# Out projection of the two attention mixers started inside their attention tails, with a split first addition, one filler less per stage and fillers in two other attentions

## The reference, cut to what matters

```python
h = rms_norm(x, norm_mix_pre[layer])
h = neighbourhood_attention(h, ...) if layer % 2 == 0 else dilated_attention(h, ...)
x = x + rms_norm(h, norm_mix_post[layer])       # attention ends with o @ w_o
h = rms_norm(x, norm_ffn_pre[layer])
x = x + rms_norm(swiglu(h, ...), norm_ffn_post[layer])
```

## Time and profile before

| | |
|---|---|
| median of 3 runs | 2242.76 us (2242.03 to 2244.25) |
| the profiled execution, its own time | 2243.23 us |
| its span, first to last instruction | 2241.4 us |
| TensorE busy | 2105.5 us, 94% |
| VectorE busy | 1391.8 us, 62% |
| ScalarE busy | 948.2 us, 42% |
| mean granted TensorE clock | 0.963 of full speed |
| moved from HBM | 338.82 MB, 152 GB/s over the span |

### The profile page before, as it was taken

One profiled execution on the slowest core, in us unless ns is written; L12 is line 12 of the kernel. 1 busy time (PEld: TensorE's weight loads), 2 busy tenths in 40 slices (PEclk: granted clock), 3 DMA queues, 4 the chain that ended last, 5 costly groups with the idle time before them and its releaser, 6 DMA issues.

```text
span 2241.4 us, 37080 instructions
## 1 busy us (share of the span) xinstructions
PE 2105.5 (94%) x15038; PEld 1942.8 (87%) x15038; DVE 1391.8 (62%) x1849; ACT 948.2 (42%) x1258; POOL 31.9 (1%) x48
## 2 busy tenths in 40 slices
PE   7989999999989999999998988999999995789998
PEld 6869988999969998998997877998899894688997
DVE  5747755655646765774667555775577456575763
ACT  4444444333444444443443334544444332544442
POOL 0000000000000000000000000000000000000000
PEclk9989999999999999999997879999999997988999
DMA  7324554343414554555530124455455552142552
GB/s 281 138 85 169 187 197 175 135 171 132 150 58 159 187 197 150 189 187 197 204 126 1 57 85 160 147 191 194 152 188 187 197 184 94 48 150 88 191 196 107
DMA packets 49788, 341.46 MB, mean 152 GB/s; under 512 B 5776, under 2 KB 6544, under 8 KB 9616
## 3 DMA queue, kind: packets, MB, share of 16 engines
q1 hardware_dynamic: 45216, 321.21, 39.6%
q10 hardware_dynamic: 4464, 18.68, 2.3%
HBM read 338.82 MB, written 1.05 MB: 152 GB/s over the span
## 4 chain that ended last, share of the span: by engine, by line
PE 83%; DVE 12%; ACT 3%; issue 2%; DMA 0%; POOL 0%; DVEq 0%; ACTq 0%; SPq 0%; POOLq 0%
PE pj L226 14%; PE pj L227 14%; PE pj L228 14%; PE acc L232 7%; PE acc L233 7%; PE acc L234 7%; DVE wlo L302 2%; PE pj L560 2%; PE pj L232 2%; PE pj L234 2%; PE pj L233 2%; PE acc L628 2%; ACT whi L295 1%; PE pj L566 1%; PE acc L616 1%
## 5 line engine op out<-in xcount | busy, mean ns | idle before, releaser
L302 DVE TENSOR_TENSOR wlo<-raw,whi 128x2048 fp32r<-128x2048 f32 x288 | 660.0, 2292 | 341.8 <-ACT whi L295 341.1
L226 PE MATMUL pj<-xh,whi 128*128 128x256 f32 x2704 | 772.6, 286 | 18.3 <-DVE wlo L312 13.4
L227 PE MATMUL pj<-xl,whi 128*128 128x256 f32 x2704 | 768.9, 284 | 0.0
L228 PE MATMUL pj<-xh,wlo 128*128 128x256 f32 x2704 | 768.9, 284 | 0.0
L295 ACT ACTIVATE whi<-raw 128x2048 fp32r<-128x2048 f32 x299 | 569.6, 1910 | 461.2 <-PE acc L234 230.9
L226 PEld LDWEIGHTS pj<-xh,whi 128*128 128x128 f32 x2704 | 522.5, 193 | 21.5 <-issue 16.0
L227 PEld LDWEIGHTS pj<-xl,whi 128*128 128x128 f32 x2704 | 522.4, 193 | 0.1
L228 PEld LDWEIGHTS pj<-xh,wlo 128*128 128x128 f32 x2704 | 522.3, 193 | 0.0
L232 PE MATMUL acc<-whi,AR 128*128 128x512 f32 x688 | 275.2, 400 | 6.7 <-DVE AR L1940 4.4
L233 PE MATMUL acc<-whi,AR 128*128 128x512 f32 x688 | 273.9, 398 | 0.0
L234 PE MATMUL acc<-wlo,AR 128*128 128x512 f32 x688 | 273.7, 398 | 0.0
(11 more groups left out here) (348 smaller groups left out, 2391.3 us busy)
## 6 DMA issues: line engine op xcount, KB each, us to landing
raw<-in_wstream SPq DMA_DIRECT2D x302, 1024.0 KB, 4.8
F<-in_gains ACTq DMA_DIRECT2D x12, 512.0 KB, 4.6
F<-in_rpb ACTq DMA_DIRECT2D x3, 1024.0 KB, 4.7
F<-in_memtok ACTq DMA_DIRECT2D x2, 1024.0 KB, 4.9
F<-in_memin ACTq DMA_DIRECT2D x2, 1024.0 KB, 7.0
F<-in_small ACTq DMA_DIRECT2D x1, 1536.0 KB, 10.5
F<-in_xin SPq DMA_DIRECT2D x2, 512.0 KB, 7.0
xt<-in_xtok SPq DMA_DIRECT2D x1, 1024.0 KB, 12.2
```

What stands on the lines that cost most here:

```text
L226: nc.tensor.matmul(o, wh, k_hi, start=first, stop=False, skip_group_check=True)
L227: nc.tensor.matmul(o, wh, k_lo, start=False, stop=False, skip_group_check=True)
L228: return nc.tensor.matmul(o, wl, k_hi, start=False, stop=last, skip_group_check=True)
L302: nc.vector.tensor_tensor(wlo[:, gs, :], raw[:, gs, :], whi[:, gs, :].bitcast(F32), ALU.subtract).then_inc(w_lo, 1)
```

## The change

In words: (a) in na and dil the sums of token half 0 go to `pj0` and `pj1` instead of `acc0` and `acc1` (`out_banks`), and the products of token half 0 with the first three weight chunks (input tiles 0 to 5, 6 matmuls each) are issued in `fill` after units 10 to 15; the fillers of these two stages are gone. The output projection then makes only banks 2 and 3 for chunks 0 to 2 (`early=3`) and all four for the last chunk. (b) `added(1, 0)` is two instructions, of 128 and of 384 columns; "x" counts 5 a stage, and TensorE turns block 0 of token half 1 after the first and blocks 1 and 2 after the second. (c) The last `keep_busy` ahead of the next stage's projection is left out. (d) `attn_pe` issues fillers in xa and dsa: ahead of each unit's transposes 3 matmuls in xa and 1 in dsa, and once after the scores of the second unit 6 and 2.

```diff
-            shares(f"s{s_}pre", "pre", {**NORM, "x": 4 if s_ else 0, "tr": KT if s_ else 0})
+            shares(f"s{s_}pre", "pre", {**NORM, "x": 5 if s_ else 0, "tr": KT if s_ else 0})
...
+        def out_banks(kind):
+
+            return [pj[0], pj[1], acc[2], acc[3]] if kind in ("na", "dil") else acc
...
-            def added(t, h):
+            def added(t, h, cols=slice(0, 512)):
                 dve.wait_ge(*at(tag, "rs", t + 1))
-                x = xt[:, t, h * 512:(h + 1) * 512]
-                nc.vector.scalar_tensor_tensor(x, tmp[2 * t + h], rsc[:, t:t + 1], x, ALU.mult, ALU.add)\
+                x = xt[:, t, h * 512:(h + 1) * 512][:, cols]
+                nc.vector.scalar_tensor_tensor(x, tmp[2 * t + h][:, cols], rsc[:, t:t + 1], x, ALU.mult, ALU.add)\
                     .then_inc(sg(nxt[0], "x"), 1)
...
-            added(1, 0)
+            added(1, 0, slice(0, P))
+            added(1, 0, slice(P, 512))
...
                 pe.wait_ge(*at(nxt, "x", 2))
-                for k in range(3):
+                turn_pe(pe, 1, 0).then_inc(sg(nxt, "tr"), 1)
+                pe.wait_ge(*at(nxt, "x", 3))
+                for k in range(1, 3):
                     turn_pe(pe, 1, k).then_inc(sg(nxt, "tr"), 1)
-                fill(pe, 4)
+                if fill is not keep_busy:
+                    fill(pe, 4)
...
-                    for b in range(4):
+                    for b in range(2 if c < early else 0, 4):
...
+        def idle(bank, n):
+
+            for _ in range(n):
+                nc.tensor.matmul(bank[:, 0:T], ident, cst[:, 0:T], start=True, stop=True)
...
             def transposes(u, U):
+                N = n_parts(U)
+                if N == 1 and u >= 2:
+                    pe.wait_ge(*at(tag, "pts", u - 1))
+                idle(parts(u, U)[0][0], U.get("idle", 0))
                 pe.wait_ge(*at(tag, "pn", u + 1))
...
             for i, U in enumerate(units):
+                if i == 0:
+                    idle(parts(u0, U)[0][0], U.get("lead", 0))
                 if i + 2 < len(units):
                     scores(u0 + i + 2, units[i + 2])
...
-                    if i >= 3 * UP:
-                        for _ in range(3 if na else 5):
-                            nc.tensor.matmul(pj[0][:, 0:T], ident, cst[:, 0:T], start=True, stop=True)
+                    if i >= 10:
+                        first_half(i - 10)
+
+                def first_half(kt):
+
+                    c, kk = divmod(kt, 2)
+                    gs = (w.g + c) % 3
+                    pe.wait_ge(w_lo, w.g + c + 1)
+                    pe.wait_ge(*at(tag, "od", kt + 1))
+                    for h in range(2):
+                        wk = slice(kk * D + h * 512, kk * D + (h + 1) * 512)
+                        mm3t(pj[h][:, :], whi[:, gs, wk], wlo[:, gs, wk], AR[:, kt, 0:P], AR[:, 8 + kt, 0:P],
+                             kt == 0, False)
...
-                out_pe(pe, w, 8, 8, tag, "od", nxt)
+                out_pe(pe, w, 8, 8, tag, "od", nxt, ob=out_banks(kind), early=3)
...
-                sp.wait_ge(*at("end", "x", i + 1))
+                sp.wait_ge(*at("end", "x", (1, 3, 4, 5)[i]))
```

More of the change, by code:

```diff
@@ L115, in build_program @@
             shares(f"s{s_}post", "post", {"g": 16, "ob": 3, "sq": 4, "mv": 2, "rs": 2})
-        shares("end", "pre", {"x": 4})
+        shares("end", "pre", {"x": 5})
         def sg(tag, n):
@@ L385, in pre_sq @@
             if tag != "s0pre":
-                act.wait_ge(*at(tag, "x", 4))
+                act.wait_ge(*at(tag, "x", 5))
             for t in range(2):
@@ L415, in post_act, with post_dve @@
                     act.wait_ge(w_used, w.g + 1)
-                nc.scalar.activation(JUNK[:, b * 512:(b + 1) * 512], acc[b][:, :], ACT.Square, accum_out=ss[:, b:b + 1])\
+                nc.scalar.activation(JUNK[:, b * 512:(b + 1) * 512], ob[b][:, :], ACT.Square, accum_out=ss[:, b:b + 1])\
                     .then_inc(sg(tag, "sq"), 1)
             act_phase(act, w, 1)
-        def post_dve(dve, w, tag, half, nxt):
+        def post_dve(dve, w, tag, half, nxt, ob):
             tmp = [Sb[:, 0, :], Sb[:, 1, :], PTb[:, 0, :], PTb[:, 1, :]]
@@ L425, in scaled @@
                 dve.wait_ge(*at(tag, "sq", b + 1))
-                link(dve, nc.vector.scalar_tensor_tensor(tmp[b], acc[b][:, :], half * D ** 0.5,
+                link(dve, nc.vector.scalar_tensor_tensor(tmp[b], ob[b][:, :], half * D ** 0.5,
                                                          GB[:, (b % 2) * 512:(b % 2 + 1) * 512], ALU.mult, ALU.mult))
@@ L473, in keep_busy, with out_pe @@
                 nc.tensor.matmul(mb[:, T:2 * T], ident, cst[:, 0:T], start=True, stop=True)
-        def out_pe(pe, w, nk, lo_at, tag, ready, nxt, beside=lambda pe, c: None, fill=keep_busy, kt0=0):
+        def out_pe(pe, w, nk, lo_at, tag, ready, nxt, beside=lambda pe, c: None, fill=keep_busy, kt0=0,
+                   ob=acc, early=0):
             post = tag + "post"
@@ L729, in two_heads @@
                              j == 0, j == 1) for a in range(2) for j in range(2)],
-                        nk=2 * T, H=2, soft=[soft(t)] * 2, grp=grp, per=2, end=t == 1)
+                        nk=2 * T, H=2, soft=[soft(t)] * 2, grp=grp, per=2, end=t == 1, idle=n_idle,
+                        lead=2 * n_idle)
         def split_out(tag, perm, o_bank):
@@ L1084, in xattn @@
                                lambda h, j: V[:, j, h * P:(h + 1) * P],
-                               lambda t: lambda S, ps: nc.vector.tensor_scalar(S, ps, P ** -0.5, None, ALU.mult), t, g)
+                               lambda t: lambda S, ps: nc.vector.tensor_scalar(S, ps, P ** -0.5, None, ALU.mult), t, g,
+                               3)
                      for g in range(2) for t in range(2)]
@@ L2134, in _ @@
                 fns[2](act, w)
-                post_act(act, w, f"s{s}post")
+                post_act(act, w, f"s{s}post", out_banks(kind))
                 if s + 1 < len(plan):
```

17 lines of the change are left out of this document (7 added, 10 removed).

## The result

The changed kernel takes 2214.38 us, the median of 4 runs (2213.06 to 2215.14), against 2243.01 (2242.03 to 2244.25) for the kernel before on the same chip: a ratio of 0.9871, with a 95% interval of 0.9856 to 0.9887. The forecast was 2215.0. Its profiled execution took 2214.05 us, 29.18 less than the 2243.23 of the profile before.

A forecast was written before the change was run, and what follows sets the result against it. TensorE, busy 94% of the span, was taken as the bound; 2243.23 - 9.5 (na) - 9.0 (dil) - 5.2 (stage ends) - 4.3 (xa) + 0.2 gave 2215.4, stated as median 2215.0. Range 2208 to 2222, with rivals 2203 to 2227.

The forecast's parts named there:

- the 8.4 us of each projection: na and dil: 36 matmuls of 0.233 us leave each output projection, bound by TensorE alone, saving 8.4 us.
- The margin at the last weight chunk: Output projection: last weight chunk ready at 7.4 us, wanted at 8.4 us, 1.0 us to spare.
- If the clock is back by about 124: na's tail: full clock by then starts the projection 1 to 2 us earlier; na gains 9.5, bounds 4.0 and 10.0.
- The two filler rows: na's tail: six filler passes take 2.56 us at 129.88 and 1.56 at 134.17, read as gapless work restoring the clock.
- dil, 0.9 gained and 0.3 lost: dil's tail: last packet brings 0.9 us forward, units 10 and 11 cost 0.3; with 8.4, dil gains 9.0.
- The stage ends: Nine stage ends: split addition and dropped filler save 0.58 us each, the filler's share 0.3; 5.2 us in all.
- both limits named: Stage end: the filler ends near 168.1, and ScalarE is busy with the chunk until 168.38.
- The fillers in xa: xa: leading fillers fill the 2.75 us idle; the second xa gains 4.3 us, the first 0; bounds 0 and 5.
- Forecast +0.1: dsa: fillers before the transposes are together 0.3 us too long, costing 0.1 us, at most 0.5.
- Rival 1: Second addition binds at stage ends (1.8 instead of 5.2) and second xa stays slow (0): 2222.6 us; 15%.
- Rival 3: Tails of na and dil: packets hold the clock at 0.50 through both, slower at 2252 us; 2%.
- Rival 2: Low-clock stretches elsewhere, as in rwrt, move, up to 14 us either way: 2207 (10%) or 2223 to 2229 (8%).

The follow-up runs named there:

- e1: The kernel before with part (a) alone: 2225.96 us.
- b1: The changed kernel with bank 2 also made early in dil, into `pj2`, 9 matmuls a packet instead of 6: 2215.28 us, ratio 0.9881.
- e7: The changed kernel with packets in units 12 to 15 only and two chunks early instead of three: 2215.49 us.
- e6: The kernel before with na's three fillers in units 10 and 11 too, dil as before: 2246.06 us.
- e2: The kernel before with the split addition alone, the filler ahead of the projection kept: 2240.86 us.
- e5: The changed kernel without the leading fillers of xa and dsa, those ahead of the transposes kept: 2217.04 us.
- e8: The changed kernel without any filler in dsa: 2216.67 us.
- e4: The kernel before with the fillers in xa and dsa alone: 2235.29 us.
- e3: The kernel before without the last filler ahead of the projection, nothing else: 2238.85 us.
- b4: The changed kernel without the od 8 wait before na's and dil's projection, plus 44 fillers in dsa: 2206.56, 2207.77 and 2212.04 us, ratio 0.9856.
- b2: The changed kernel with bank 2 also made early in both na and dil: 2213.60 us, ratio 0.9874.
- b7: The kernel of b4 with fillers after unit 8 in both tails, 10 in na and 8 in dil: 2208.65 us, ratio 0.9850.

## Why the prediction was right, point by point

- **What bounds it, and the 8.4 us of each projection.** Right: 22.27 us became 13.87 in na and 22.26 became 13.87 in dil, and e1 shows the same with part (a) alone. The margin at the last weight chunk was forecast at 1.0 us and is 1.16; b1 used it up and found 1.53 us of idle.
- **"If the clock is back by about 124 ... the projection starts 1 to 2 us earlier".** The condition held, the worth didn't: the clock was back at 124.6, but the projection started 0.75 us earlier (142.44 for 143.19), of which 0.39 came ahead of the tail; the tail gained 0.36. The reason given, that gapless work brings the clock back, fits the traces (seven builds with such work and three without, in the table of e7), and e6 shows what the earlier return is worth with fillers alone, 0.8 us. The two filler rows on which I relied couldn't show it, since e7 and e2 got the clock back early with no such work. The term that was mis-sized is the gain behind the packets: unit 10 alone became 2.2 us longer (its packet ran at half clock, 118.42 to 124.53 for one unit that took 3.91 before), which ate most of what the earlier clock gave back. The 9.17 for a forecast of 9.5 is within the bounds of 4.0 and 10.0, and 8.40 of it is the projection.
- **dil, 0.9 gained and 0.3 lost.** The tail gained 1.74, not 0.6. The stretch at half clock in it was half as long as before (3.4 us for 6.9), some 1.7 us by an estimate. In e1, e5 and e8, which have the same dil code and a stretch of 6.8 us, the tail takes 34.37, 34.50 and 34.57 us for 35.06: 0.5 to 0.7 gained, as forecast. Ahead of the tail, stretches that had moved cost 1.1 us (one from 425.0 to 428.4 is new). So the mechanism was right, and that this build came to 9.08 for a forecast of 9.0 is partly luck: e1's dil gained 6.76.
- **The stage ends.** 0.55 us each for a forecast of 0.58, and both limits named (the filler, the end of ScalarE's chunk) are seen in the rows. The share that I gave the filler, 0.3, was wrong as a share: alone it is worth 0.20, the split alone 0, and 0.35 is there only for both. The Trainium skill's fixed latency for an instruction on SBUF operands (VectorE: DVE Perf Modes, TRN2 errata) agrees with the trace: two parts take 0.13 us more than one whole (0.88 against 0.75), and the product loop didn't feel it.
- **The fillers in xa.** Right in size and place: -4.68 for -4.3, and e4 gives the same alone. That the leading fillers would do it was half the truth (2.6 of 4.7 us, e5). The stretch is gone in all eight builds with both kinds of filler, so it wasn't luck.
- **dsa.** Forecast +0.1; measured -1.19. e8 shows that the fillers there do nothing. The gain is luck: it lies ahead of the attention, in one stretch at half clock of the input projection (3.5 us for 6.8, the rows above). e3 and e4, with no edit there either, have 3.3 and 3.7 us by others.
- **The rivals.** Rival 1 (binding second addition, slow second xa) would have shown in rows that came out the other way. Rival 3 had its condition, packets at half clock, for one packet in na and none in dil. Rival 2 is real and was given too small a chance for a single stage: stretches moved by several us in every build. In the changed kernel they happened to add up to little: rwrt, its place in the forecast, stayed within 0.02 us. About the placement of such stretches the Trainium skill (TensorE: Matmul & The Clock Gate, Part 1) says that the watch on activity runs free of the kernel's start. The times here show something narrower: the executions of one build lie within 1.5 to 5.6 us of each other, while the same stage differs by up to 8 us between builds (rwrt, e1 against b4).

## What to carry to other kernels

Work taken out of a phase that is bound by TensorE alone is worth its full duration, if it goes into slots where TensorE idled or ran fillers; what it costs there depends on the clock at that place, so price it at both levels. Before crediting the end of a stretch at half clock to the work in it, see how the stretch lies in other builds. Two small edits on one chain can be worth nothing apart and something together: look which wait ends second before dividing a gain between them. And when an experiment with one edit moves stages that it doesn't touch, compare stage by stage and take the stretches at half clock off first, or their luck is read as the edit's effect.

## What the runs showed of the hardware that was not expected

- Stretches at half clock (1.2 GHz) move between builds in code that is the same. rwrt took 6.94 us less in e1, 6.31 less in e7 and 1.00 more in b4; the part of s9 ahead of its attention went down by 0 to 3.7 us; dil's input projection has one in the changed kernel (425.0 to 428.4), e1, e6 (431.7 to 438.6), e7, e8, b1, b2 and b7, and none there before or in e2 to e5 and b4. This is larger than what parts (b) or (c) are worth, and full times of single executions can't rank them.
- The half clock in na's tail follows an idle of 4.7 us ahead of the scores of unit 11: with 20 filler passes in it the clock stayed at 1.00 in b7. How long it lasts isn't set by the work behind it alone: 118.3 to 131.9 in the kernel before, 119.1 to 126.0 in e7, with the same instructions up to there. Work without gaps in units 10 and 11 goes with an end by 125.2, nothing there with an end at 131 or later, unless the fall comes at 119 or later (the table of e7). What sets the time of the fall stays open.
- Fillers while TensorE would have idled for some 20 us (dsa, b4) kept the clock up, and gave 1.1 us in the attention behind them.
